# The MLA output projection of a fused three-mixer block: who loads the angles, which engine scales the residual, and where ten tiles of powers and the first lags stand

## The reference

```python
def _mla_output(o_lat, gate, w_uv, w_out):              # layer 0, end
    v = jnp.einsum('bnhc,chv->bnhv', o_lat, w_uv).reshape(b, n, MLA_WIDTH)   # width 2048
    return (v * jax.nn.silu(gate)) @ w_out              # to width 1024
...
x = _layernorm(DEEPNORM_ALPHA * x + gt[:, None] * y_lat, ln_g[i], ln_b[i])
...
# layer 1, per group: powers of a complex decay, times B and times C
b_bar = ((lam_bar - 1.0) / lam)[..., None] * bmat
powers = jnp.exp(lam_dt[None] * jnp.arange(1, S5_CHUNK + 1)[:, None, None])
```

## Time and profile before

| what | value |
|---|---|
| median of 3 runs (lowest to highest) | 2107.43 us (2101.98 to 2112.67) |
| profiled execution: its own time, its span | 2106.93 us, 2105.2 us |
| PE busy over the span | 1979.7 us (94%) |
| VectorE, ScalarE, GpSimd busy | 1520.4, 909.1, 521.8 us |
| the chain that ended last, by engine | PE 76%, DVE 9%, DMA 5%, ACT 5% |
| output product, last head's end to PE's last matmul of it | about 1091 to 1228.5 us |

### The profile page before, as it was taken

How to read it: one execution, slowest core, us unless ns; L and a number is a source line. 1 busy time by engine, 2 the same in 40 slices (tenths; PEclk the granted TensorE clock), 3 DMA queues, 4 the chain that set the end, 5 groups by cost and what they waited for, 6 DMA issues and landing times.

```text
span 2105.2 us, 42824 instructions
## 1 busy us (share of the span) xinstructions
PE 1979.7 (94%) x17574; PEld 1616.2 (77%) x17574; DVE 1520.4 (72%) x2111; ACT 909.1 (43%) x1532; POOL 521.8 (25%) x419
## 2 busy tenths in 40 slices
PE   7999898899999999999998979999999899999996
PEld 6787787787886566555578957888877799999885
DVE  3366665368994688788868966888893798898844
ACT  3335543334324444444454456555443543443423
POOL 2553221140015999300001221111121111111000
PEclk9999999899999999999999989999999999999998
DMA  9221333332452122111138866999975423333321
GB/s 367 81 96 65 123 144 142 126 131 85 160 190 86 69 87 91 66 63 56 73 134 302 315 230 171 306 308 310 326 232 180 135 96 111 101 101 111 141 90 40
DMA packets 127506, 317.89 MB, mean 151 GB/s; under 512 B 12128, under 2 KB 59104, under 8 KB 120912
## 3 DMA queue, kind: packets, MB, share of 16 engines
q1 hardware_dynamic: 112032, 243.14, 34.3%
q0 software_dynamic: 10672, 53.14, 7.0%
q10 hardware_dynamic: 4608, 18.88, 2.4%
HBM read 238.69 MB, written 76.41 MB: 150 GB/s over the span
## 4 chain that ended last, share of the span: by engine, by line
PE 76%; DVE 9%; DMA 5%; ACT 5%; issue 4%; POOL 1%; SPq 0%; ACTq 0%; DVEq 0%; POOLq 0%
PE psum L523 15%; PE psum L3761 13%; PE psum L2016 7%; PE psum L3185 6%; PE psum L2631 5%; DMA made_table<-table_made 4%; PE psum L2594 3%; PE psum L1195 3%; PE psum L2606 3%; PE psum L3355 2%; PE psum L336 2%; PE psum L3305 2%; PE psum L3414 2%; PE psum L2682 1%; PE psum L2620 1%
## 5 line engine op out<-in xcount | busy, mean ns | idle before, releaser
L3185 PE MATMUL psum<-h,u_w 128*128 128x256 f32 (+1 forms) x768 | 157.8, 351 | 7.1 <-DVE h L3115 5.1
L523 PE MATMUL psum<-h_split,in_w 128*128 128x512 f32 x600 | 139.0, 391 | 1.5 <-POOL in_w L512 1.5
L3185 PEld LDWEIGHTS psum<-h,u_w 128*128 128x128 f32 x768 | 119.1, 192 | 26.4 <-issue 11.5
L3718 POOL TENSOR_TENSOR ring<-ring 128x1024 f32<-128x1024 f32 x16 | 54.2, 3386 | 318.7 <-DVE xT L3712 318.7
L523 PEld LDWEIGHTS psum<-h_split,in_w 128*128 128x128 f32 x600 | 111.9, 188 | 27.2 <-ACT prev L859 2.1
L512 POOL TENSOR_TENSOR u_w<-ring,u_w 128x512 fp32r<-128x512 f32 x42 | 54.2, 1291 | 272.8 <-ACT u_w L500 236.7
L505 DVE TENSOR_TENSOR w_split<-ring,w_split 128x512 fp32r<-128x512 f32 x54 | 40.7, 755 | 84.4 <-ACT w_split L500 84.2
L2016 PE MATMUL psum<-x_high,ring_split 128*128 128x512 f32 x272 | 101.1, 393 | 0.0
L2631 PE MATMUL psum<-area,ckv_tm 128*128 128x512 f32 (+1 forms) x256 | 100.4, 545 | 0.0
L2729 DVE TENSOR_REDUCE early<-psum 128x1 f32<-128x768 f32 (+1 forms) x96 | 74.8, 780 | 31.8 <-PE psum L2606 29.1
L512 POOL TENSOR_TENSOR in_w<-ring,in_w 128x512 fp32r<-128x512 f32 x50 | 78.0, 1560 | 79.1 <-ACT in_w L500 76.9
(11 more groups left out here) (527 smaller groups left out, 5271.4 us busy)
## 6 DMA issues: line engine op xcount, KB each, us to landing
ring<-in_s_glu SPq DMA_DIRECT2D x64, 512.0 KB, 3.3
ring<-in_w_mod SPq DMA_DIRECT2D x48, 512.0 KB, 5.3
c_pow<-made_c_pow SPq DMA_DIRECT2D x32, 576.0 KB, 5.1
ring<-in_s_in SPq DMA_DIRECT2D x32, 512.0 KB, 6.8
b_pow<-made_b_pow SPq DMA_DIRECT2D x15, 1024.0 KB, 10.4
ring<-in_w_in SPq DMA_DIRECT2D x25, 512.0 KB, 3.3
made_table<-table_made ACTq DMA_DIRECT2D x16, 768.0 KB, 4.7
table<-made_table SPq DMA_DIRECT2D x32, 384.0 KB, 6.4
```

The costliest lines, as they stand in the source:

```text
L523: ins = nc.tensor.matmul(out, rounded(buffer(u, w)[:, ks]), values(x, k), start=(first and k == 0 and n == 0), stop=(last and k == UNIT_K ...
L3185: ins = nc.tensor.matmul(o, rounded(u_w[:, u % 4, w, kk * P:(kk + 1) * P]), h3_part(x, k)[:, a:a + size], start=(k == 0 and n == 0), stop= ...
L3718: nc.gpsimd.tensor_tensor(left_plain(i, "S3"), left_plain(i, "A11"), left_plain(i, "S3"), ALU.subtract).then_inc(pool_done, 1)
```

## The change

- Angles 0 and 1 are issued by ScalarE at the head of `mla_out_act`; angles 2 to 15 by SP, between loads of weights, after a wait for the store of table `m - 2`. Angle and table 15 use half 1 of `b_pow_out` (in `area`), after b powers 13 are stored.
- ScalarE: one table per weight unit, behind `mla_out_w_act(i)`; unit 2 is rounded ahead of the last slice of `gate2_high`, unit 3 ahead of table 0. The multiplication of `h2` by ALPHA_2 moves from VectorE to ScalarE (`h2_scaled_act`).
- EARLY_B_POW 4 to 5, five steps a head: the added one stands in pair 1. Ten tiles, 60 steps, four a unit, stay beside the product; the residual of tile `m - 1` stands after 8 steps and 2 weight units of VectorE's program.
- The first lags move on PE from behind the output product to behind `ln2.spread`, on ScalarE and VectorE into `s5_start` at `k == 2`; their second bank is 5 in place of 2. SP loads `b_bar` and `c_pow` 0 at `s5_in` 4 in place of 1, and `c_pow` 1 and `b_pow` right behind.

```diff
@@ -67,9 +67,9 @@
 CTX_AHEAD = 3
 LATE_C_POW = 10
 LATE_HEAD = 3
-EARLY_B_POW = 4
+EARLY_B_POW = 5
 B_POW_HEAD = 9
-B_POW_A_HEAD = 4
+B_POW_A_HEAD = 5
...
             pool.wait_ge(pool_done, pool_count.up())
             pool.dma_start(io["angle"][m], angle_out[m % 2]).then_inc(angle_stored[m % 2], 16)
 
-        def angle_load_act(act, m):
-            if m >= 2:
-                act.wait_ge(table_stored[m % 2], 16 * (m // 2))
-            act.dma_start(table_made[:, m % 2, N_TABLE // 2:N_TABLE], io["angle"][m]).then_inc(angle_loaded[m % 2], 16)
+        def table_room(m):
+            return area[:, N_B_POW:N_B_POW + N_TABLE] if m == KE - 1 else table_made[:, m % 2, :]
+
+        def angle_load(engine, m):
+            loaded = angle_last if m == KE - 1 else angle_loaded[m % 2]
+            engine.dma_start(table_room(m)[:, N_TABLE // 2:N_TABLE], io["angle"][m]).then_inc(loaded, 16)
+
+        def angle_sync(sp, m):
+            if m == KE - 1:
+                sp.wait_ge(b_pow_stored[1], 16 * (KE // 2 - 1))
+            else:
+                sp.wait_ge(table_stored[m % 2], 16 * (m // 2))
+            angle_load(sp, m)
 
         def table_act(act, m):
 
-            if m == 0:
-                angle_load_act(act, 0)
-            if m + 1 < KE:
-                angle_load_act(act, m + 1)
-            cosine, sine = table_made[:, m % 2, 0:N_TABLE // 2], table_made[:, m % 2, N_TABLE // 2:N_TABLE]
-            act.wait_ge(angle_loaded[m % 2], 16 * (m // 2 + 1))
+            cosine, sine = table_room(m)[:, 0:N_TABLE // 2], table_room(m)[:, N_TABLE // 2:N_TABLE]
+            if m == KE - 1:
+                act.wait_ge(angle_last, 16)
+            else:
+                act.wait_ge(angle_loaded[m % 2], 16 * (m // 2 + 1))
             nc.scalar.activation(cosine, sine, ACT.Abs).then_inc(act_done, 1)
             act.wait_ge(act_done, act_count.up())
             nc.scalar.activation(sine, sine, ACT.Sin, scale=6.283185).then_inc(act_done, 1)
             act_count.up()
             nc.scalar.activation(cosine, cosine, ACT.Sin, bias=eps[:, 4:5], scale=-6.283185).then_inc(act_done, 1)
             act.wait_ge(act_done, act_count.up("s5", "table", m))
-            act.dma_start(io["table"][m], table_made[:, m % 2, :]).then_inc(table_stored[m % 2], 16)
+            act.dma_start(io["table"][m], table_room(m)).then_inc(table_stored[m % 2], 16)
 
         def tables_pool(pool):
...
@@ -2885,14 +2894,14 @@
                 if pair == 2 and h == HEADS - 1:
                     gate2_low_dve(dve, 5)
                 if pair == 1:
-                    b_pow_early_dve(dve, early + 1, early + 2)
+                    b_pow_early_dve(dve, early + 1, early + 3)
                 normalize_dve(dve, n + 2 * pair + 1)
                 if pair == 0 and late_here:
                     c_pow_steps_dve(dve, late, late + 1)
                 if pair == 0:
                     b_pow_early_dve(dve, early, early + 1)
                 if pair == 2:
-                    b_pow_early_dve(dve, early + 2, early + 4)
+                    b_pow_early_dve(dve, early + 3, early + 5)
                 if pair == 0 and h >= HEADS - 2:
                     mla_out_w_dve(dve, h - (HEADS - 2))
                 if pair == 0 and h == HEADS - 1:
...
@@ -2986,14 +2995,25 @@
             for m in range(1, KD):
                 mla_out_steps_pe(pe, m, 0, KE)
 
+        def h2_scaled_act(act, m):
+            if m == 0:
+                act.wait_ge(x_back, 2 * 16)
+            nc.scalar.activation(h2[:, m, :], h2[:, m, :], ACT.Copy, scale=ALPHA_2).then_inc(act_done, 1)
+            act_count.up("h2_scaled", m)
+
         def mla_out_act(act):
+            for m in range(2):
+                angle_load(act, m)
+            mla_out_w_act(act, 2)
             gate2_high_act(act, KE - 1)
             made = 0
-            for i in range(2 * KD):
-                mla_out_w_act(act, i + 2)
-                while made < min(KE, i + 2):
-                    table_act(act, made)
-                    made += 1
+            for i in range(3, 2 * KD):
+                mla_out_w_act(act, i)
+                if i - 3 < KD:
+                    h2_scaled_act(act, i - 3)
+                for m in range(made, i - 1 if i < 2 * KD - 1 else KE):
+                    table_act(act, m)
+                    made = m + 1
 
         B_POW_BESIDE = KE - 1 - EARLY_B_POW
...
@@ -3005,6 +3025,7 @@
             h3_gain_dve(dve)
             def residual(m):
                 dve.wait_ge(*at("mla_out", m))
+                dve.wait_ge(*at("h2_scaled", m))
                 for i, (a, b) in enumerate(((0, CTX), (CTX, TC))):
...
@@ -3013,17 +3034,14 @@
 
             for m in range(KD):
                 first = 2 * m * B_POW_A_SLOT
-                mla_out_w_dve(dve, 2 * m + 2)
-                b_pow_beside_dve(dve, first, first + 2)
-                if m > 0:
+                if m == 0:
+                    mla_out_w_dve(dve, 2)
+                else:
+                    b_pow_beside_dve(dve, first - B_POW_A_SLOT, first)
+                    mla_out_w_dve(dve, 2 * m + 2)
                     residual(m - 1)
-                b_pow_beside_dve(dve, first + 2, first + B_POW_A_SLOT)
+                b_pow_beside_dve(dve, first, first + B_POW_A_SLOT)
                 mla_out_w_dve(dve, 2 * m + 3)
-                if m == 0:
-                    dve.wait_ge(x_back, 2 * 16)
-                v.tensor_scalar(h2[:, m, :], h2[:, m, :], ALPHA_2, None, ALU.mult).then_inc(dve_done, 1)
-                dve.wait_ge(dve_done, dve_count.up())
-                b_pow_beside_dve(dve, first + B_POW_A_SLOT, first + 2 * B_POW_A_SLOT)
             residual(KD - 1)
...
@@ -3085,9 +3103,13 @@
         h3_cols = lambda i, k, v: h3_gain[:, i, k, v:v + 1]
 
         def s5_start_act(act):
+            act.wait_ge(table_stored[1], 16 * KE // 2)
             for u in range(4):
                 u_w_act(act, u)
+            b_split_act(act, 0)
             for k in range(KD):
+                if k == 2:
+                    lags_act(act, 0)
                 if k >= 2:
                     act.wait_ge(*at("s5", "h3", k - 2))
...
@@ -3117,6 +3139,8 @@
 
             for k in range(KD):
                 ln2.scale_dve(dve, k)
+                if k == 2:
+                    lags_dve(dve, 0)
                 if k >= 2:
                     dve.wait_ge(*at("s5", "h3", k - 2))
                 tmp3 = h3_tmp[k % 2].rearrange("p (s c) -> p s c", s=STEP)
...
 
         def lag_bank(m, d, a, b):
-            return bank((4, 7 if m > 0 else 2)[d], a, b)
+            return bank((4, 7 if m > 0 else 5)[d], a, b)
...
@@ -4053,7 +4077,13 @@
                         sp.wait_ge(b_pow_stored[i], 16 * ((EARLY_B_POW + 1 - i) // 2))
                     sp.dma_start(h2[:, :, CTX:TC], io["x_kept"]).then_inc(x_back, 16)
                     sp.dma_start(h2[:, :, 0:CTX], io["ctxT"]).then_inc(x_back, 16)
-                if n == slot_of[("s5_in", 1)]:
+                for m in range(2, KE - 3):
+                    if n == slot_of[("mla_out", m + 3)]:
+                        angle_sync(sp, m)
+                for m in range(KE - 3, KE):
+                    if n == slot_of[("s5_in", m - (KE - 3))]:
+                        angle_sync(sp, m)
+                if n == slot_of[("s5_in", 4)]:
                     for who in ("pe", "act", "dve", "pool"):
                         sp.wait_ge(*at("end", "heads", who))
                     for made in table_stored:
@@ -4062,7 +4092,6 @@
                         b_bar_sync(sp, tile)
                     for h in range(2):
                         c_pow_sync(sp, 0, h)
-                if n == slot_of[("s5_in", 2)]:
                     sp.wait_ge(*at("mla_out", KD - 1))
                     for h in range(2):
...
@@ -4141,11 +4170,11 @@
                 head_pe(pe, h)
             phase_end(pe, pe_count, "heads")
             mla_out_pe(pe)
-            lags_pe(pe, 0)
             ln2.mean_pe(pe)
             ln2.var_pe(pe)
             phase_end(pe, pe_count, "mla")
             ln2.spread_pe(pe)
+            lags_pe(pe, 0)
             s5_pe(pe)
             phase_end(pe, pe_count, "s5", mark=False)
             gates_pe(pe)
```

More of the change, by code:

```diff
@@ L224, in build @@
         x_back = memory.enter_context(nc.semaphore("x_back"))
+        angle_last = memory.enter_context(nc.semaphore("angle_last"))
         lam_loaded = memory.enter_context(nc.semaphore("lam_loaded"))
@@ L4172, in _ @@
             mla_out_act(act)
-            b_split_act(act, 0)
-            lags_act(act, 0)
             ln2_std_act(act)
@@ L4203, in _ @@
             mla_out_dve(dve)
-            lags_dve(dve, 0)
             ln2.centre_dve(dve)
```

## The result

| | before | after |
|---|---|---|
| first comparison, median (lowest to highest, runs) | 2106.16 us (2101.98 to 2112.67, 4) | 2086.21 us (2084.59 to 2087.77, 4) |
| ratio, 95% interval | | 0.9898 (0.9875 to 0.9921) |
| second comparison, same two kernels | 2108.74 us (2098.60 to 2125.61, 28) | 2090.59 us (2088.34 to 2105.84, 9) |
| ratio, 95% interval | | 0.9931 (0.9908 to 0.9955) |
| profiled execution: its own time, its span | 2106.93, 2105.2 us | 2087.72, 2085.9 us |

Its interval puts the change at 16.6 to 26.3 us, where I had 14.4. The second comparison has an interval of 9.5 to 19.4 us: 14.6 by its ratio (0.0069 x 2108.74), 18.2 by its medians. My 14.4 lies in the second interval and not in the first.

A forecast was written before the change was run, and what follows sets the result against it. PE, 94% busy, was taken as the bound, with 14.9 us of the output product above it. Terms -14.9 + 1.1 + 0 - 1.5 + 0.9 = -14.4 took the median 2107.43 to 2093.0 us, range 2088 to 2103.

The forecast's parts named there:

- Bound of the product: Seven tiles of the output product: PE's waits and slow matmuls go, reaching 16.87 us a tile, -14.9 us.
- VectorE sets the pace: Later product tiles before the change: VectorE needs 17.9 us a tile against PE's 16.87, so residuals come late.
- Start: Start of the product: two issues and weight unit 2 ahead of the last gated slice cost +1.1 us (0.5 to 1.9).
- Heads: Six heads: the added fifth step is covered by VectorE's idle time, 0 us; without cover 3.4, at most 7.6.
- Lags out of the way: Between output product and mean: moving the first lags away gives -1.5 us (-0.5 to -2.0).
- Lags in h3: The h3 stage: ScalarE's copies and VectorE's small operations for the lags add +0.9 us (0.4 to 1.4).
- Last table: Angle and table 15 after b powers 13 are stored: c_pow has 8 us slack, cost 0, up to +1.
- Angles on SP's queue: Angles issued behind SP's weight loads: cost 0 as long as table m - 2 is stored by then.
- Rival C: SP's program: a late table store holds up weight loads, 20.5 us a tile, 2118 us; chance 0.06.
- A: Output product: some waits for residuals or units 2 to 5 stay, -6 us, 2101.5 us; chance 0.12.
- B: Heads: the added step is not covered, +3.4 to +7.6 us, about 2098 us; chance 0.08.
- D: S5 start: tables, c_pow or first weights some 14 us late give the gain back, about 2107 us; chance 0.06.

The follow-up runs named there:

- u7_round_first: The kernel before with each weight unit rounded one place earlier on ScalarE (units 2 and 3 ahead of table 0): product 127.18 us, run 2104.99 us.
- u8_old_tables: The changed kernel with angles issued by ScalarE again and tables 0 and 1 ahead of weight unit 3: product 124.87 us.
- u1_four_early: The changed kernel with four tiles of b powers in the heads instead of five: 2094.92 us, ratio 0.9933; product 121.3 us.
- u2_scale_dve: The changed kernel with the scaling by ALPHA_2 back on VectorE: product 118.29 us.
- u4_start: The changed kernel with the last slice of gated values rounded ahead of two angle issues and weight unit 2: start 8.88 us, run 2083.12 us.
- u5_lags_early: The changed kernel with the first lags back between output product and mean: 2106.59 us, ratio 0.9990.
- u6_lags_late: The changed kernel with the first lags behind the whole h3 stage: h3 38.34 us, the stage behind it 837.6 us.
- c_after: The changed kernel measured and profiled again without an edit: 2090.59 us, ratio 0.9931.
- best: The changed kernel with the edits of u4_start and u6_lags_late together: 2088.30 us, ratio 0.9905.
- u3_angles_act: The changed kernel with angles 2 to 15 issued by ScalarE again behind waits for table stores: product 119.4 us, mean stage 10.8 us.
- c_before: The kernel before measured and profiled again without an edit: median 2105.15 us, ratio 0.9986 against 28 other runs of itself.

## Why the prediction was off, point by point

*Bound of the product: right.* I had 14.9 us; it is 14.86 in the first pair. The two causes that I named are both real: the rounding behind the waits (6.0 by u7_round_first, 6.6 by u8_old_tables from the other side), and VectorE's part (the other 8.3 to 8.9). Of that part the fifth tile in the heads counts 3.0 (u1_four_early), the scaling 0 (u2_scale_dve). Some 5 to 6 us belong to neither alone. They can be the two together, or the place of the residual, which moved ahead of two steps; the prediction gave that no price and no run tried it by itself. That no residual is late in u1_four_early, by my sum at 17.3 us a tile, speaks for the place; so my "VectorE sets the pace" is shown for the weights, not for the residuals. VectorE's 14.6 us a tile are 102.2 in seven, measured 102.62. That they meet so closely is luck in part: there are 60 steps in the seven tiles and not 56, of 1.31 us and not 1.36.

*Start: right.* +1.1 forecast, +1.05 measured, and u4_start takes it back whole. ScalarE began the last slice 6.32 us behind the last `o_lat`, where my sum has 6.3, and VectorE the rest of unit 2 at 8.56, before 7.52.

*Heads: right.* Heads 9 to 14 take 162.73 us, before 162.90.

*Lags out of the way: right, and undersold.* The mean stage is 1.28 and 1.00 shorter in the two pairs (forecast 1.5). What I didn't say is that the gain of the product hangs on this move: `c_pow` lands 13.8 us behind the end of a product at full speed (u5_lags_early; 14.2 in after), where my sum has 1225.4 - 1213.7 = 11.7, or 10.6 with the later start. The lags want it 19.2 us behind, so 5.0 to 5.4 us of my 8 are there. Without the move the change is worth nothing.

*Lags in h3: right.* +0.9 forecast, +0.86 measured in the first pair, 0.9 back in u6_lags_late.

*Last table: wrong.* I weighed it against `c_pow` alone. In ScalarE's program the squares of the normalization stand behind it, and they want ScalarE about 5 us behind the product's end, with a table load of 1.28 us between. The slack against them is 1.06 us in one trace of after, and 1.6 us are missing in another (h3 40.89 against 39.25). So it costs 0 or 1.6. In c_after the store of b powers 13 took 10.6 us, against 7.4 in after, and angle 15 went out 2.1 us later. In `best` it went out no later than in after, but took 5.6 us to land where it took 4.0, and the squares were due 1.6 us earlier. Both the store and the load can use up the slack.

*Angles on SP's queue: right in size, by a thinner cover than I gave.* Store, angle and table took 5.4 + 6.2 + 2.8 = 14.4 us where I had 11.6, against the 16.87 of two units. Rival C did not come. After the row of SP's 138.8 us I had cited the Trainium skill ("DMA: Bandwidth & Descriptors", Anatomy of one DMA) for the sequencer that sits out a wait. SP's row of 11.4 us and ScalarE's 54.0 in u3_angles_act agree with it: waits for the same stores cost PE nothing on SP, and on ScalarE 1.1 us in the product and 7.2 in the mean.

*Rivals.* A, B and D are not seen in the traces of after: no residual is late, no head is longer, and h3 starts on time but for table 15.

*The step that failed* is the one from the sum to the time: "three runs of before lie 10.7 apart", from which I took 3 us either way. The profiled execution of before is one draw, and so is each of after. In fifteen traces of thirteen programs that run the same instructions up to the first head, the end of the first block lies between 399.5 and 412.1 us. The first pair had 409.5 and 401.2, the second 403.7 and 403.5. By the sum of terms the change is -14.4; the traces give -14.2 and -13.1 for the touched stages. The first comparison gave -19.95 in medians of four, the second -18.2 in medians or -14.6 by its ratio. So the terms hold; whether up to some 4 us more come with the change stays open. That the second comparison lies nearer to my number doesn't make the first one right. The range should have been some 6 us either way for a comparison of few runs. Its lower end had a slip too: my own bounds add to -14.9 + 0.5 - 2.0 + 0.4 = -16.0, not -17.0.

What makes the scatter is shown in part. Over the fifteen traces the time of the first block goes with the time that TensorE's clock spent at its lower level (1.2 of 2.4 GHz) in it: 13.7 to 37.5 us, and a line through them rises by 0.34 us per us, with a correlation of 0.86. The first pair of traces had 37.5 and 13.7 us of it, the second 23.9 in both. Whole executions show the same: the four of after in the first comparison had a granted clock of 0.981 to 0.985, the nine of the second 0.976 to 0.982; over the forty of before in the second comparison, 0.972 to 0.983, time falls as the clock rises, with a correlation of -0.82. The Trainium skill ("TensorE: Matmul & The Clock Gate", Terms) gives a penalty of half the throttled time, which makes 0.5 us per us as an estimate for this case. The traces' 0.34 is below it. That these dips cause the longer time is the likely reading, since the same instructions run, but no run here could set the clock. Why one execution has more of them than another stays open.

## What to carry to other kernels

When a stall goes, walk every engine's program behind the stalled work and ask of each wait there how much it has to spare against the new, earlier end: here a transfer that was 0.8 us late would have been 13.8 late and eaten nearly the whole gain, had the lags not moved too, and one table on ScalarE is still at the edge. A wait for a store belongs on a queue with nothing urgent behind it, and a rounding that feeds PE belongs ahead of any wait. And when a prediction starts from one profiled execution, compare stages that the change doesn't touch before believing a difference: here 5 us of 19.3 came from them.

## What the runs showed of the hardware

- The same instructions take 399.5 to 412.1 us for the first block in fifteen traces, with the granted clock of the RWKV part between 0.93 and 0.97.
- PE's clock fell to its lower level behind waits of 3.86 us, 3.38 (u8_old_tables, 0.59 over 4 us, and c_before), 2.74 (u7_round_first), 2.28 (u6_lags_late) and 2.18 (c_before), and not behind 3.19 nor 1.97 (c_after). The length of one wait doesn't decide. In u6_lags_late the fall (0.57 over 4 us) made two dozen matmuls 1.6 us longer, more than the 0.9 by which h3 was shorter.
- A switch of ScalarE's function table took 1.28 us with 0.39 idle ahead, and it stands on the path when the squares are late.
- In the product of after, loads and stores landed later than in that of before (5.4 against 4.7 us for a table's store, 6.2 against 4.1 for an angle), at 304 GB/s against 297. What made them later was not tested.
